# Token rows gathered to partitions 0 to 31 and 64 to 95 with a 128-entry index column, in a mixture-of-experts kernel

## The chip, the cores and the metric

The kernel runs on one core of a Trainium2 chip. Engines are named as in the profile: PE is TensorE's matmul, PEld its weight load, DVE is VectorE, ACT ScalarE, POOL GpSimd, SP SyncE. Sixteen DMA engines move data for the core. The metric is the device time of one execution in microseconds (us), as the median over several runs.

## The reference

Two transformer blocks over 512 tokens of width 1024, in float32. The first has sparse and differential attention and an MLP. The second has windowed attention, an mLSTM branch and, at its end, a mixture of 32 experts. Only this last part is touched:

```python
# each token picks one group of 8 experts and its 2 best experts in it
order = jnp.argsort(expert_ids)              # 1024 assignments, sorted by expert
...
xs = xt[row_tok].reshape(nblk, MOE_BLOCK, D) # rows of the normed input h
def expert_block(args):
    xb, e = args
    return (jax.nn.silu(xb @ w_gate[e]) * (xb @ w_up[e])) @ w_down[e]
...
y = jnp.zeros((T, D)).at[row_tok].add(ys * row_w[:, None])
```

Each expert has 6.3 MB of weights: `gate` and `up` (1024 x 512 each) and `down` (512 x 1024).

## The kernel before

The first 1,220 us, about, hold everything ahead of the experts. The router then sorts the 1024 assignments into blocks of 64 places (`BLK`), one block per expert and a second one for up to four experts: 36 blocks (`STATIC`), worked through in the order of the list `ORDER`. A block is seldom full. Its tokens stand on consecutive places, whose start turns by 5 places from block to block (`TURN`).

**Tables.** `place_choice` (DVE) builds one-hot matrices, `place_hot` (place of each assignment in its block) and `tok_weight` (block, with the token's number minus 1024, and its weight). `all_slots` (PE, line 1629) multiplies them and gets, for each of the 64 places and each block, the token number and the gate weight in PSUM. `all_rows` (DVE, lines 2968, 2914 and 2915) copies the weights to `slot_weight` and makes `row_ids`: the token number, or for an empty place a number beyond the last token.

**Gather.** For each block from the third on, POOL copies one column of `row_ids` to `idcol` (line 929) and issues an indirect DMA (line 921), which fetches one row of 4 KB from `h_scratch` in HBM for each index into `xs[0:64, s]` (the tile is `stage`; s is 0 or 1 in turn). An index out of bounds fetches nothing. The gather of block n+5 is issued when PE has turned the rows of block n+3, and the first three ahead of the loop. The first two blocks are made by matmuls, without a gather.

**Blocks.** For block n PE computes gate and up (line 1641: `xsT` with 1024 x 512 weights, the two products in the two halves of PE's columns), turns the gathered rows of block n+1 (line 1635, `turn_tokens`, partitions 0 to 95 of `xs` into 96 columns of PSUM, of which DVE's `turned_tokens` takes columns 0 to 63), computes down for block n-1 (line 1658), and turns the hidden rows (line 1649). DVE line 2982 makes the hidden rows. ACT lines 2121 and 2123 write the result rows to `ys` (the tile is `smb`).

**Scatter.** `add_rows` (POOL, line 943) adds the 64 rows of `ys` to the output in HBM with an accumulating indirect DMA. One is issued per block, each after the one before has landed. For the last block, `spread` issues another gather ahead of the last scatter, for a loop over overflow blocks, which does not run with these inputs.

**Weights.** SP streams the experts' weights through eleven places of 2 MB in the order of `LOADS`, each as soon as PE has used up the piece that lay there. All go through one queue, q1 in the profile. POOL's indirect DMAs go through q0.

Of the kernel before, what the change touches and what calls it, by code (L numbers as in the profile page):

```python
# [23 lines left out]
I32 = mybir.dt.int32  # L24
ALU = mybir.AluOpType
# [3 lines left out]
P = 128  # L29
D = 1024  # L30
SEQ = 512
NT = SEQ // P
# [15 lines left out]
BLK = 64  # L48
# [8 lines left out]
STATIC = NE + DOUBLES  # L57
BLOCKS = STATIC + MAXJOBS + 2
# [51 lines left out]
def build(nc, io, out):  # L110
    ctx = ExitStack()
    with ctx:
        def sb(name, shape, dt=F32):
            return ctx.enter_context(nc.sbuf_tensor(name, shape, dt))
# [5 lines left out]
        ps = ctx.enter_context(nc.psum_tensor("ps", [P, 8, 512], F32))  # L120
# [30 lines left out]
        small = sb("small", [P, 640])  # L151
        cur = [0]
# [14 lines left out]
        row_gain = col(KT)  # L167
# [122 lines left out]
        wpos = sb("wpos", [P, 2, NT])  # L290
        tokid = sb("tokid", [P, 2, NT])
        iot = sb("iot", [P, 2 * BLK + 1])
        idcol = sb("idcol", [BLK, 4], I32)
        tables = fmask[0:1, 0:MAXJOBS + NE].bitcast(I32)
        jobs, placed = tables[:, 0:MAXJOBS], tables[:, MAXJOBS:]
        njobs = sb("njobs", [1, 1], I32)
# [29 lines left out]
        place_hot = gb[:, 0:2 * NT * BLK].rearrange("p (n r) -> p n r", n=2 * NT)  # L326
        tok_weight = flat_s[:, 0:4 * NT * BLOCKS].rearrange("p (n b) -> p n b", n=2 * NT)
# [3 lines left out]
        xs = stage  # L331
        ys = flat_s[0:64, :].rearrange("p (s d) -> p s d", s=2)
        xsT = [v.rearrange("p (k t) -> p k t", k=KT) for v in (gb[:, 512:1024], cmask[:, :])]
        hidT = ptb[:, 1, 0:256].rearrange("p (k t) -> p k t", k=4)
        slot_weight = ptb[64:128, 1, 256:256 + BLOCKS]
        sgate, hid = flat_s[64:128, 1024:1536], flat_s[64:128, 1536:2048]

        row_ids = small[0:BLK, cur[0]:cur[0] + BLOCKS].bitcast(I32)
        id_work = small[0:BLK, cur[0] + BLOCKS:cur[0] + 2 * BLOCKS]
        assert cur[0] + 2 * BLOCKS <= 640  # L340

        h_dram = nc.dram_tensor("h_scratch", (SEQ, D), F32, kind="Internal").ap()
# [82 lines left out]
        idT_done, ids_ready, job_ready = sem("idT_done"), sem("ids_ready"), sem("job_ready")  # L425
# [6 lines left out]
        idcol_ready = sem("idcol_ready")  # L432
# [33 lines left out]
        b = C_P2  # L466
# [340 lines left out]
        def _(pool):  # L807
# [110 lines left out]

            def gather_tokens(s):
                pool.sem_inc(fetches, 1)  # L920
                pool.indirect_dma_start(out=xs[0:BLK, s, :], out_offset=None, in_=h_dram,
                                        in_offset=bass.IndirectOffsetOnAxis(ap=idcol[:, s:s + 1], axis=0),
                                        bounds_check=SEQ - 1, oob_is_err=False).then_inc(gather[s], 16)

            nth = [0]

            def index_column(col_, b):
                nth[0] += 1
                pool.tensor_copy(idcol[:, col_:col_ + 1], row_ids[:, b:b + 1]).then_inc(idcol_ready, 1)
                pool.wait_ge(idcol_ready, nth[0])  # L930

            def block_at(n):
                return ORDER[n][1] if n < STATIC else n

            def fetch(n, s, turned):
                if turned > 0:
                    pool.wait_ge(ex["xt"], turned)
                index_column(s, block_at(n))
                gather_tokens(s)

            def add_rows(s):
                pool.sem_inc(fetches, 1)
                pool.indirect_dma_start(out=out[0], out_offset=bass.IndirectOffsetOnAxis(ap=idcol[:, 2 + s:3 + s], axis=0),
                                        in_=ys[0:BLK, s, :], in_offset=None, bounds_check=SEQ - 1, oob_is_err=False,
                                        compute_op=ALU.add).then_inc(rows_out, 16)

            def spread(n):
                last = n == STATIC - 1
                if last:
                    pool.wait_ge(rows_out, 16 * (n - 1))  # L950
                    index_column(2 + n % 2, block_at(n))
                    fetch(STATIC + 1, 0, STATIC - 1)
                    pool.wait_ge(last_rows, 1)
                pool.wait_ge(ex["ys"], n + 1)
                if not last:
                    index_column(2 + n % 2, block_at(n))
                if n:
                    pool.wait_ge(rows_out, 16 * n)
                add_rows(n % 2)

            for n in range(2, 5):
                fetch(n, n % 2, n - 3)
            pool.wait_ge(out_store, 16 * NT)
            for n in range(STATIC):
                spread(n)
                if n + 5 <= STATIC:
                    fetch(n + 5, (n + 5) % 2, n + 2)
            base = nth[0]
            pool.wait_ge(job_ready, 1)
            n = pool.value_load(njobs[0:1, 0:1], min_val=0, max_val=MAXJOBS)  # L970
            with pool.If(n > 0):
                with pool.Fori(0, n) as j:
                    pool.wait_ge(ex["xt"], j + STATIC)
                    pool.tensor_copy(idcol[:, 0:1], row_ids[:, bass.ds(j + (STATIC + 2), 1)]).then_inc(idcol_ready, 1)
                    pool.wait_ge(idcol_ready, j * 2 + (base + 1))
                    gather_tokens(0)
                    pool.wait_ge(ex["ys"], j + (STATIC + 1))
                    pool.tensor_copy(idcol[:, 2:3], row_ids[:, bass.ds(j + STATIC, 1)]).then_inc(idcol_ready, 1)
                    pool.wait_ge(idcol_ready, j * 2 + (base + 2))
                    pool.wait_ge(rows_out, j * 16 + 16 * STATIC)  # L980
                    add_rows(0)
# [3 lines left out]
        def _(pe):  # L985
# [80 lines left out]
            for g in range(BESIDE1):  # L1066
                if G1[g][0] != "wi":
                    dense1(g, (0, 1))
                else:
                    group(bank1(g), wi_done, 1)  # L1070
                    pe.wait_ge(swap_done, 5)
                    for i in range(NT):
                        ins = pe.transpose(ps[:, bank1(g), 8 * i:8 * i + 8], wi_rows[:, i * P:(i + 1) * P],
                                           ident[64:72, 64:72])
# [77 lines left out]
            for a in range(N_STEPS + 3):  # L1152
# [8 lines left out]
                if piece(a):  # L1161
                    g, part = piece(a)
# [346 lines left out]
            for half in range(2):  # L1509
# [5 lines left out]
                for j in range(4):  # L1515
                    for br_ in range(2):
                        bank = (2 * bo + br_) % 4
                        group(bank, u_done, bo + 1)
                        for k in range(4):
                            ins = pe.matmul(ps[:, bank, :],  # L1520
                                            ring[c % 2][:, br_ * 2048 + k * 512 + j * P:br_ * 2048 + k * 512 + (j + 1) * P],
                                            yT[:, 4 + k, :] if br_ else oT[:, k, :], start=(k == 0), stop=(k == 3))
# [82 lines left out]
            for k in range(KT):  # L1605
                for i in range(NT):
                    ins = pe.matmul(ps[:, k // 4, (k % 4) * P:(k % 4 + 1) * P], x[:, i, k * P:(k + 1) * P],
                                    first_hot[:, 2 * i:2 * i + 2, :], start=(i == 0), stop=(i == NT - 1))
# [4 lines left out]
            for i in range(NT):  # L1613
                ins = pe.matmul(ps[:, 3, 0:3], first_hot[:, 2 * i:2 * i + 2, :].rearrange("p e r -> p (e r)"), r_first_w[:, i, :],
                                start=(i == 0), stop=(i == NT - 1))
# [9 lines left out]
            def all_slots():  # L1625
                for c in range(2):
                    pe.wait_ge(slots_ready, c + 1)
                    for n in range(NT * c, NT * (c + 1)):
                        ins = pe.matmul(ps[0:BLK, 7, 0:2 * BLOCKS], place_hot[:, n, :], tok_weight[:, n, :],
                                        start=(n == 0), stop=(n == 2 * NT - 1))  # L1630
                ins.then_inc(idT_done, 1)

            def turn_tokens(s):
# [43 lines left out]
            for n, (q, _) in enumerate(ORDER):  # L1677
                s = n % 2
# [28 lines left out]
            n = pe.value_load(njobs[0:1, 0:1], min_val=0, max_val=MAXJOBS)  # L1707
# [436 lines left out]
        def _(dve):  # L2144
            steps = [0]

            def then(ins):

                steps[0] += 1
                ins.then_inc(dv, 1)  # L2150
                dve.wait_ge(dv, steps[0])

            def bc(col_, n):

                return col_.unsqueeze(len(col_.shape)).broadcast_to(list(col_.shape) + [n])
# [682 lines left out]
            root(3)  # L2838
            dve.wait_ge(root_ready, NT)

            dve.memset(r_two[:, 0:FIXED], 0.0)
            dve.tensor_copy(r_near[:, 0:FIXED], iot[:, 0:FIXED])
            dve.tensor_scalar(block_start, iot[:, 0:BLOCKS], float(BLK), None, ALU.mult)
# [66 lines left out]
                                         ps[:, half, :].rearrange("p (k t) -> p k t", k=4)[:, :, 0:BLK],  # L2910
                                         bc(gcol[:, 6, 4 * half:4 * half + 4], BLK), ALU.mult)

            def token_ids(dst, src, work_):
                then(dve.tensor_scalar(work_, src, float(-SEQ), float(-SEQ), ALU.is_ge, ALU.mult))
                return dve.scalar_tensor_tensor(out=dst, in0=src, scalar=float(2 * SEQ), in1=work_, op0=ALU.add, op1=ALU.add)

            cnt = ps[:, 7, 0:NE]
            then(dve.tensor_tensor(more, bc(cnt, NBLK - 1), block_start[:, 1:NBLK].unsqueeze(1).broadcast_to([P, NE, NBLK - 1]),
                                   ALU.is_gt))
# [45 lines left out]
            dve.sem_inc(job_ready, 1)  # L2965
            def all_rows():
                dve.wait_ge(idT_done, 2)
                dve.tensor_copy(slot_weight, ps[0:BLK, 7, BLOCKS:2 * BLOCKS])
                token_ids(row_ids, ps[0:BLK, 7, 0:BLOCKS], id_work).then_inc(ids_ready, 1)

            def turned_tokens(s, n):
                dve.wait_ge(ex["xt"], n)
                for half in range(2):
                    ins = dve.tensor_tensor(xsT[s][:, 4 * half:4 * half + 4, :],
                                            ps[:, half, 0:4 * 96].rearrange("p (k t) -> p k t", k=4)[:, :, 0:BLK],
                                            bc(row_gain[:, 4 * half:4 * half + 4], BLK), ALU.mult)
                ins.then_inc(ex["xT"], 1)

            def hidden(e, weight):
# [81 lines left out]
```

## Time and profile before

| | |
|---|---|
| median of 3 runs | 1709.47 us (1708.0 to 1710.34) |
| span of the profiled execution | 1706.2 us |
| own time of that execution | not on the page; the median is 3.3 us above the span |
| PE busy | 1639.4 us (96%) |
| DVE, ACT, POOL busy | 736.9, 388.6, 189.6 us |
| q1 (weights) | 287.40 MB, 43.9% of 16 engines' span |
| q0 (POOL's DMAs) | 12.90 MB, 3.7% |

The span runs from the first to the last instruction of the profiled execution. A queue's share is the time that its packets took, over 16 DMA engines and the stretch that is looked at. It is a mean over stages: in the last 450 us the DMA engines are far busier than over the whole span.

### The profile page before, as it was taken

The page shows a single profiled execution, that of the slowest core. Times are in us where ns is not written, and L with a number is a line of the kernel's source. Part 1 is how long each engine was busy: PE and PEld are TensorE (multiplying, and loading weights), DVE is VectorE, ACT ScalarE, POOL GpSimd, SP SyncE. Part 2 cuts the span into 40 slices and gives each one's busy share as a digit, 9 for nine tenths or more (in the row PEclk, how much of TensorE's full clock was granted, in tenths as well). Part 3 has the DMA queues.
Part 4 walks back from the last instruction along what each step waited for, and adds up shares of the span by engine and source line. Part 5 has one row for each costly group of instructions (what it writes and reads, how often), then busy time and mean ns, then how long its engine had stood idle before and what let it go on. Part 6 is the DMA issues. An engine that isn't in the chain of part 4 may idle for free.

```text
span 1706.2 us, 18047 instructions
## 1 busy us (share of the span) xinstructions
PE 1639.4 (96%) x6990; PEld 951.3 (56%) x6990; DVE 736.9 (43%) x1520; ACT 388.6 (23%) x823; POOL 189.6 (11%) x206
## 2 busy tenths in 40 slices
PE   7999999999999999999999999999999998988986
PEld 4444454578888888865444778645533333333332
DVE  3386886465444544452775355243422121111111
ACT  4443754410000000032454233102211111110110
POOL 1000000000000000010000414132022222111211
PEclk9999999999999999999999999999999999999998
DMA  5531114030222122222111113647899999999996
GB/s 186 126 72 49 50 50 148 1 111 1 99 99 88 61 99 99 99 63 99 50 50 50 50 50 99 201 148 281 315 384 395 401 402 403 395 396 412 395 404 239
DMA packets 72257, 303.61 MB, mean 178 GB/s; under 512 B 10669, under 2 KB 11826, under 8 KB 59756
## 3 DMA queue, kind: packets, MB, share of 16 engines
q1 hardware_dynamic: 63856, 287.40, 43.9%
q0 software_dynamic: 7568, 12.90, 3.7%
q10 hardware_dynamic: 748, 2.15, 0.3%
q8 instruction: 56, 0.92, 0.2%
q14 instruction: 29, 0.24, 0.0%
HBM read 297.56 MB, written 15.73 MB: 184 GB/s over the span
## 4 chain that ended last, share of the span: by engine, by line
PE 87%; DMA 9%; DVE 2%; issue 1%; another core or an unknown queue 0%; ACT 0%; POOL 0%; POOLq 0%; SPq 0%; DVEq 0%; ACTq 0%
PE ps L1193 11%; PE ps L1237 11%; PE ps L1641 11%; PE ps L1061 9%; DMA W<-in_w_expert_up 8%; PE ps L1334 7%; PE ps L1658 6%; PE ps L1481 5%; PE ps L1097 3%; PE ps L1057 3%; PE ps L1520 3%; PE ps L1546 3%; PE ps L1345 2%; PE ps L1116 1%; PE ps L1635 1%; PE ps L1013 1%
## 5 line engine op out<-in xcount | busy, mean ns | idle before, releaser
L2982 DVE SCALAR_TENSOR_TENSOR smb<-smb,ptb,ps 64x512 f32<-64x512 f32 x34 | 38.3, 1126 | 291.6 <-ACT smb L2115 291.6
L1641 PE MATMUL ps<-W,gb 128*64 128x512 f32 x480 | 140.3, 645 | 15.9 <-DMA W<-in_w_expert_up 15.9
L1061 PE MATMUL ps<-W 128*128 128x512 f32 (+1 forms) x336 | 149.3, 596 | 1.4 <-DVE W L2172 1.4
L1641 PE MATMUL ps<-W,cmask 128*64 128x512 f32 x480 | 129.3, 599 | 6.1 <-DMA W<-in_w_expert_up 3.1
L1334 PE MATMUL ps<-W 128*128 128x512 f32 x272 | 124.0, 606 | 1.9 <-DVE yT L2630 1.9
L1193 PE MATMUL ps<-yT,W 128*128 128x256 f32 x512 | 113.0, 379 | 0.0
L1658 PE MATMUL ps<-W,ptb 128*64 128x512 f32 x464 | 107.7, 606 | 1.4 <-DVE ptb L2988 1.4
L1237 PE MATMUL ps<-W,mix 128*128 128x256 f32 x496 | 108.5, 379 | 0.0
L1193 PEld LDWEIGHTS ps<-yT,W 128*128 128x128 f32 x512 | 97.3, 190 | 13.2
L1061 PEld LDWEIGHTS ps<-W 128*128 128x128 f32 (+1 forms) x336 | 61.2, 188 | 74.9 <-issue 72.9
L1237 PEld LDWEIGHTS ps<-W,mix 128*128 128x128 f32 x496 | 94.2, 190 | 12.8
L1237 PE MATMUL ps<-W 128*128 128x256 f32 x400 | 88.0, 379 | 0.0
L1334 PEld LDWEIGHTS ps<-W 128*128 128x128 f32 x272 | 50.6, 192 | 66.4 <-issue 63.5
L1641 PEld LDWEIGHTS ps<-W,gb 128*64 128x64 f32 x480 | 43.0, 148 | 78.8 <-issue 78.2
L1868 ACT ACTIVATE smb<-ps 128x512 f32<-128x512 f32 x10 | 6.0, 596 | 349.8 <-PE ps L1237 185.3
L1193 PE MATMUL ps<-W 128*128 128x256 f32 x384 | 85.5, 379 | 0.0
L1237 PEld LDWEIGHTS ps<-W 128*128 128x128 f32 x400 | 76.0, 190 | 10.3
L2115 ACT ACTIVATE smb<-ps 64x512 f32<-64x512 f32 x34 | 20.1, 590 | 261.9 <-PE ps L1641 261.9
L1641 PEld LDWEIGHTS ps<-W,cmask 128*64 128x64 f32 x480 | 42.7, 137 | 65.0 <-issue 64.3
L1193 PEld LDWEIGHTS ps<-W 128*128 128x128 f32 x384 | 72.8, 190 | 9.8
L1658 PEld LDWEIGHTS ps<-W,ptb 128*64 128x64 f32 x464 | 31.3, 138 | 55.5 <-issue 50.8
L1794 ACT ACTIVATE yT<-ps 32x512 f32<-32x512 f32 x82 | 48.3, 589 | 44.2 <-PE ps L1061 43.4
(476 smaller groups left out, 2426.3 us busy)
## 6 DMA issues: line engine op xcount, KB each, us to landing
W<-in_w_expert_up SPq DMA_DIRECT2D x27, 2048.0 KB, 40.7
W<-in_w_expert_gate SPq DMA_DIRECT2D x24, 2048.0 KB, 37.6
W<-in_w_expert_down SPq DMA_DIRECT2D x24, 2048.0 KB, 44.4
W<-in_w_in SPq DMA_DIRECT2D x16, 2048.0 KB, 7.7
W<-in_w_up SPq DMA_DIRECT2D x8, 2048.0 KB, 8.2
W<-in_w_down SPq DMA_DIRECT2D x8, 2048.0 KB, 7.9
W<-in_w_out SPq DMA_DIRECT2D x4, 2048.0 KB, 7.9
yT<-in_w_expert_down SPq DMA_DIRECT2D x4, 2048.0 KB, 39.8
```

Source lines behind the costliest of these rows:

```text
L1057: ins = pe.matmul(ps[:, bank, :], hT[:, k, j * P:(j + 1) * P], wv[:, k, :], start=(k == 0), stop=(k == KT - 1))
L1061: ins = pe.matmul(ps[0:n, bank, :], wv[:, k, j * P:j * P + n], hT[:, k, :], start=(k == 0), stop=(k == KT - 1))
L1097: ins = pe.matmul(ps[:, bank, :], lhs[:, k, i * P:(i + 1) * P], ring_view(c, KT, 512)[:, k, :], start=(k == 0), stop=(k == 7))
L1193: ins = pe.matmul(ps[:, bank, 256 * j:256 * j + 256], lhs[:, k, j * P:(j + 1) * P], rhs[:, k, :], start=(j == 0 and k == 0), stop=(j == 1 ...
L1237: ins = pe.matmul(ps[:, bank, 256 * t:256 * t + 256], lhs[:, k, t * P:(t + 1) * P], rhs[:, k, :], start=(q == 0 and t == 0 and k == 0), st ...
L1334: ins = pe.matmul(ps[:, bank, :], wv[:, k, j * P:(j + 1) * P], hT[:, k, :], start=(k == 0), stop=(k == KT - 1))
L1481: ins = pe.matmul(ps[:, bank, 256 * j:256 * j + 256], lhs[:, k, j * P:(j + 1) * P], rhs[:, k, :], start=(j == 0 and k == 0), stop=(j == 1 ...
L1520: ins = pe.matmul(ps[:, bank, :], ring[c % 2][:, br_ * 2048 + k * 512 + j * P:br_ * 2048 + k * 512 + (j + 1) * P], yT[:, 4 + k, :] if br_ ...
L1546: ins = pe.matmul(ps[:, bank, :], lhs[:, k, t * P:(t + 1) * P], rhs[:, k, :], start=(k == 0), stop=(k == 3))
L1641: ins = pe.matmul(ps[64 * part:64 * part + 64, 2, :], xsT[s][:, k, :], w[part][:, k, :], start=(k == 0), stop=(k == KT - 1))
L1658: ins = pe.matmul(ps[64 * half:64 * half + 64, 4, :], hidT[:, k, :], w[:, k, half * 512:(half + 1) * 512], start=(k == 0), stop=(k == 3))
L1794: ins = act.activation(yT[32 * r:32 * r + 32, 4 + swaps % 2, :], ps[32 * (r ^ 1):32 * (r ^ 1) + 32, bank, :], ACT.Copy)
```

## The change

The gathers write 128 partitions' worth of entries instead of 64. Places 0 to 31 of a block go to partitions 0 to 31, places 32 to 63 to partitions 64 to 95. The entries for partitions 32 to 63 and 96 to 127 hold an index out of bounds, so nothing is fetched for them. For this `all_slots` computes the two halves of the places into two groups of PSUM partitions, `all_rows` works on the two groups apart (`gather_ids`, filled with 1024 beforehand) and copies them together for the scatter (`row_ids`) and the weights. DVE takes columns 0 to 31 and 64 to 95 of the turned rows. The scatter is as before, from 64 partitions.

```diff
@@ tiles @@
-        idcol = sb("idcol", [BLK, 4], I32)
+        idcol = sb("idcol", [P, 4], I32)
...
-        row_ids = small[0:BLK, cur[0]:cur[0] + BLOCKS].bitcast(I32)
-        id_work = small[0:BLK, cur[0] + BLOCKS:cur[0] + 2 * BLOCKS]
+        gather_ids = small[:, cur[0]:cur[0] + BLOCKS].bitcast(I32)
+        id_work = small[:, cur[0] + BLOCKS:cur[0] + 2 * BLOCKS]
+        row_ids = small[0:BLK, cur[0] + BLOCKS:cur[0] + 2 * BLOCKS].bitcast(I32)
@@ POOL @@
-                pool.indirect_dma_start(out=xs[0:BLK, s, :], out_offset=None, in_=h_dram,
+                pool.indirect_dma_start(out=xs[:, s, :], out_offset=None, in_=h_dram,
                                         in_offset=bass.IndirectOffsetOnAxis(ap=idcol[:, s:s + 1], axis=0),
                                         bounds_check=SEQ - 1, oob_is_err=False).then_inc(gather[s], 16)
...
-            def index_column(col_, b):
+            def token_column(s, b):
                 nth[0] += 1
-                pool.tensor_copy(idcol[:, col_:col_ + 1], row_ids[:, b:b + 1]).then_inc(idcol_ready, 1)
+                pool.tensor_copy(idcol[:, s:s + 1], gather_ids[:, b:b + 1]).then_inc(idcol_ready, 1)
+                pool.wait_ge(idcol_ready, nth[0])
+
+            def row_column(s, b):
+                nth[0] += 1
+                pool.tensor_copy(idcol[0:BLK, 2 + s:3 + s], row_ids[:, b:b + 1]).then_inc(idcol_ready, 1)
                 pool.wait_ge(idcol_ready, nth[0])
...
             pool.wait_ge(out_store, 16 * NT)
+            pool.wait_ge(ids_ready, 2)
             for n in range(STATIC):
                 spread(n)
@@ PE @@
                     for n in range(NT * c, NT * (c + 1)):
-                        ins = pe.matmul(ps[0:BLK, 7, 0:2 * BLOCKS], place_hot[:, n, :], tok_weight[:, n, :],
-                                        start=(n == 0), stop=(n == 2 * NT - 1))
+                        for part in range(2):
+                            ins = pe.matmul(ps[64 * part:64 * part + 32, 7, 0:2 * BLOCKS], place_hot[:, n, 32 * part:32 * part + 32],
+                                            tok_weight[:, n, :], start=(n == 0), stop=(n == 2 * NT - 1))
@@ DVE @@
+            dve.tensor_scalar(gather_ids, iot[:, 0:BLOCKS], 0.0, float(2 * SEQ), ALU.mult, ALU.add)
...
             def all_rows():
                 dve.wait_ge(idT_done, 2)
-                dve.tensor_copy(slot_weight, ps[0:BLK, 7, BLOCKS:2 * BLOCKS])
-                token_ids(row_ids, ps[0:BLK, 7, 0:BLOCKS], id_work).then_inc(ids_ready, 1)
+                quarters = (slice(0, 32), slice(64, 96))
+                for at in quarters:
+                    ins = dve.tensor_scalar(id_work[at], ps[at, 7, 0:BLOCKS], float(-SEQ), float(-SEQ), ALU.is_ge, ALU.mult)
+                then(ins)
+                for at in quarters:
+                    ins = dve.scalar_tensor_tensor(out=gather_ids[at], in0=ps[at, 7, 0:BLOCKS], scalar=float(2 * SEQ), in1=id_work[at],
+                                                   op0=ALU.add, op1=ALU.add)
+                ins.then_inc(ids_ready, 1)
+                dve.wait_ge(ids_ready, 1)
+                for part, at in enumerate(quarters):
+                    dve.tensor_copy(slot_weight[32 * part:32 * part + 32], ps[at, 7, BLOCKS:2 * BLOCKS])
+                    ins = dve.tensor_copy(row_ids[32 * part:32 * part + 32], gather_ids[at])
+                ins.then_inc(ids_ready, 1)
...
                 for half in range(2):
-                    ins = dve.tensor_tensor(xsT[s][:, 4 * half:4 * half + 4, :],
-                                            ps[:, half, 0:4 * 96].rearrange("p (k t) -> p k t", k=4)[:, :, 0:BLK],
-                                            bc(row_gain[:, 4 * half:4 * half + 4], BLK), ALU.mult)
+                    ins = dve.tensor_tensor(xsT[s][:, 4 * half:4 * half + 4, :].rearrange("p k (q t) -> p k q t", q=2),
+                                            ps[:, half, 0:4 * 96].rearrange("p (k q t) -> p k q t", k=4, q=3)[:, :, 0:3:2, :],
+                                            bc(bc(row_gain[:, 4 * half:4 * half + 4], 2), 32), ALU.mult)
```

On POOL, behind the last of the router's helper sums and up to the second scatter, the kernel before has these instructions (line, operation, destination and sources, shape):

```order
L929 COPY idcol<-small 64x1
L921 DMA stage<-h_scratch,idcol 64x1024
L929 COPY idcol<-small 64x1
L921 DMA stage<-h_scratch,idcol 64x1024
L929 COPY idcol<-small 64x1
L921 DMA stage<-h_scratch,idcol 64x1024
L929 COPY idcol<-small 64x1
L943 DMA out_x<-smb,idcol 512x1024
```

In the changed kernel they are:

```order
L930 COPY idcol<-small 128x1
L922 DMA stage<-h_scratch,idcol 128x1024
L930 COPY idcol<-small 128x1
L922 DMA stage<-h_scratch,idcol 128x1024
L930 COPY idcol<-small 128x1
L922 DMA stage<-h_scratch,idcol 128x1024
L935 COPY idcol<-small 64x1
L949 DMA out_x<-smb,idcol 512x1024
```

The order is the same, and the gathers and their index columns have 128 entries. The same pattern goes on through the loop.

On DVE, behind the second `place_choice` and ahead of the second block's hidden rows, there are in the kernel before (`ptb` holds `slot_weight`, `small` the ids):

```order
L2997 TENSOR_TENSOR gb<-ptb,iot 128x256
L2968 COPY ptb<-ps 64x54
L2914 TENSOR_SCALAR small<-ps 64x54
L2915 SCALAR_TENSOR_TENSOR small<-ps,small 64x54
L2982 SCALAR_TENSOR_TENSOR smb<-smb,small,ps 64x128x4
```

and in the changed kernel:

```order
L3013 TENSOR_TENSOR gb<-ptb,iot 128x256
L2975 TENSOR_SCALAR small<-ps 32x54 x2
L2978 SCALAR_TENSOR_TENSOR small<-ps,small 32x54 x2
L2983 COPY ptb<-ps 32x54
L2984 COPY small<-small 32x54
L2983 COPY ptb<-ps 32x54
L2984 COPY small<-small 32x54
L2998 SCALAR_TENSOR_TENSOR smb<-smb,small,ps 64x128x4
```

Three operations become eight. The ids now come ahead of the weights' copies.

On PE, between the first block's down and the second block's gate and up, the kernel before has

```order
L1658 MATMUL ps<-W,ptb 64x512 x8
L1629 MATMUL ps<-smb,gb 64x108 x8
L1641 MATMUL ps<-W,cmask 64x512 x16
```

and the changed kernel

```order
L1666 MATMUL ps<-W,ptb 64x512 x8
L1637 MATMUL ps<-smb,gb 32x108 x16
L1649 MATMUL ps<-W,cmask 64x512 x16
```

`all_slots` has twice as many matmuls of half the width, at the same place.

## Rows read from the trace of the kernel before

**Rows 1.** Page: its first line.

```profile
span 1706.2 us, 18047 instructions
```

**Rows 2.** Stretch 1500 to 1550: length, busy engines, clock, DMA share, GB/s.

```profile
1500.00:1550.00 50.00, 40.29 (x200) 15.76 (x196) 7.74 (x15) 6.52 (x11) 9.92 (x15) 0.97 1.02 406
```

**Rows 3.** PE's waits from 1238 us on: total us, times, longest.

```profile
PE ps L1641 <- DMA W<-in_w_expert_up: 27.8, 11, 5.0
```

**Rows 4.** Chain that ended last, near the end: start, us, what.

```profile
1660.50 4.88 another core or an unknown queue
1665.51 9.21 PE ps L1641 x32
1679.66 7.02 PE ps L1641 x32
```

**Rows 5.** DMA queues from 1248 to 1672: packets, MB, share of 16 engines.

```profile
q1 hardware_dynamic: 11245, 161.84, 93.5%
q0 software_dynamic: 5155, 7.32, 7.3%
```

**Rows 6.** DMA queues from 1442 to 1447.

```profile
q1 hardware_dynamic: 147, 2.15, 100.3%
q0 software_dynamic: 10, 0.00, 0.1%
```

**Rows 7.** DMA queues from 1177 to 1183.

```profile
q1 hardware_dynamic: 178, 2.55, 100.0%
```

**Rows 8.** POOL from 1345 to 1352: start, us, what.

```profile
1345.37 0.99 POOL L921 DMA_INDIRECT stage<-h_scratch,idcol  x1 [0.86 <-POOL idcol L929]
1350.32 1.45 POOL L943 DMA_INDIRECT out_x<-smb,idcol  x1 [0.92 <-POOL idcol L929]
```

**Rows 9.** DMA queues from 1349 to 1354.

```profile
q1 hardware_dynamic: 94, 1.39, 83.9%
q0 software_dynamic: 74, 0.26, 15.9%
```

**Rows 10.** DMA queues from 1355 to 1359.

```profile
q1 hardware_dynamic: 99, 1.43, 84.2%
q0 software_dynamic: 79, 0.15, 19.6%
```

**Rows 11.** DMA queues from 358 to 361, POOL loading `gb`.

```profile
q1 hardware_dynamic: 499, 1.00, 87.0%
q0 software_dynamic: 50, 0.20, 18.5%
```

**Rows 12.** DMA queues from 1168 to 1173.

```profile
q1 hardware_dynamic: 991, 2.00, 104.9%
```

**Rows 13.** The same chain, two earlier pieces.

```profile
1190.69 1.02 PE ps L1575 x15
1227.92 1.38 PE ps L1629 x15
```

**Rows 14.** A stretch with DMA engines idle; SP's next issue.

```profile
1236.00:1237.00 1.00, 1.00 (x10) 0.70 (x8) 0.00 (x0) 0.68 (x1) 0.00 (x0) 1.00 0.00 0
1236.45 0.34 SPq L777 DMA_DIRECT2D W<-in_w_expert_gate  x1
```

**Rows 15.** Gathers into `stage`, 1225 to 1262: us from issue to landing.

```profile
DMA to landing us min/median/max: 3.0/8.7/9.7
```

**Rows 16.** Timeline: first gather's issue on POOL, its reader on PEld.

```profile
1231.31 1.06 POOL L921 DMA_INDIRECT stage<-h_scratch,idcol  x1 [0.96 <-POOL idcol L929]
1236.19 0.70 PEld L1635 LDWEIGHTS ps<-ident,stage 96*128 96x128 f32 x8 [0.81 <-DMA stage<-h_scratch,idcol]
```

**Rows 17.** Timeline from 1696 us: ACT and POOL.

```profile
1696.23 0.59 ACT L2121 ACTIVATE smb<-ps 64x512 f32<-64x512 f32 x1 [3.85 <-PE ps L1658]
1696.28 1.01 POOL L921 DMA_INDIRECT stage<-h_scratch,idcol  x1 [0.90 <-POOL idcol L929]
1698.05 1.42 POOL L943 DMA_INDIRECT out_x<-smb,idcol  x1 [0.76 <-issue]
```

More of the change, by code:

```diff
@@ L937, in fetch @@
                     pool.wait_ge(ex["xt"], turned)
-                index_column(s, block_at(n))
+                token_column(s, block_at(n))
                 gather_tokens(s)
@@ L942, in add_rows @@
                 pool.sem_inc(fetches, 1)
-                pool.indirect_dma_start(out=out[0], out_offset=bass.IndirectOffsetOnAxis(ap=idcol[:, 2 + s:3 + s], axis=0),
+                pool.indirect_dma_start(out=out[0], out_offset=bass.IndirectOffsetOnAxis(ap=idcol[0:BLK, 2 + s:3 + s], axis=0),
                                         in_=ys[0:BLK, s, :], in_offset=None, bounds_check=SEQ - 1, oob_is_err=False,
@@ L950, in spread @@
                     pool.wait_ge(rows_out, 16 * (n - 1))
-                    index_column(2 + n % 2, block_at(n))
+                    row_column(n % 2, block_at(n))
                     fetch(STATIC + 1, 0, STATIC - 1)
@@ L955, in spread @@
                 if not last:
-                    index_column(2 + n % 2, block_at(n))
+                    row_column(n % 2, block_at(n))
                 if n:
@@ L973, in _ @@
                     pool.wait_ge(ex["xt"], j + STATIC)
-                    pool.tensor_copy(idcol[:, 0:1], row_ids[:, bass.ds(j + (STATIC + 2), 1)]).then_inc(idcol_ready, 1)
+                    pool.tensor_copy(idcol[:, 0:1], gather_ids[:, bass.ds(j + (STATIC + 2), 1)]).then_inc(idcol_ready, 1)
                     pool.wait_ge(idcol_ready, j * 2 + (base + 1))
@@ L977, in _ @@
                     pool.wait_ge(ex["ys"], j + (STATIC + 1))
-                    pool.tensor_copy(idcol[:, 2:3], row_ids[:, bass.ds(j + STATIC, 1)]).then_inc(idcol_ready, 1)
+                    pool.tensor_copy(idcol[0:BLK, 2:3], row_ids[:, bass.ds(j + STATIC, 1)]).then_inc(idcol_ready, 1)
                     pool.wait_ge(idcol_ready, j * 2 + (base + 2))
@@ L2911, in first_rows @@
                                          bc(gcol[:, 6, 4 * half:4 * half + 4], BLK), ALU.mult)
-            def token_ids(dst, src, work_):
-                then(dve.tensor_scalar(work_, src, float(-SEQ), float(-SEQ), ALU.is_ge, ALU.mult))
-                return dve.scalar_tensor_tensor(out=dst, in0=src, scalar=float(2 * SEQ), in1=work_, op0=ALU.add, op1=ALU.add)
             cnt = ps[:, 7, 0:NE]
```

## The prediction

> **What bounds the kernel now.** First the stage in which the change acts. The experts run from about 1220 us to the end. Here the 16 DMA engines are never free: a stretch of it shows a DMA share of 1.01, while PE works 40 of 50 us [rows 2]. Then who waits: PE stands 27.8 us in 11 waits at line 1641 for `up` weights [rows 3], and the chain that ended last passes through such a wait of 4.88 us at 1660.50 [rows 4] and then holds nothing but the last two blocks, some 30 us of PE work, and their scatters. So the arrival of the last weights sets the end. A microsecond less of work per DMA engine before 1660 is a microsecond off the span, until PE's waits are used up.
>
> Next, what that work is. From 1248 to 1672 us q1, the weights, moved 161.84 MB at 93.5% [rows 5]. I turn such a row into engine time per MB: share x stretch x 16 engines / MB. The stage as a whole: 0.935 x 424 x 16 / 161.84 = 39.2 us. Where POOL moves no rows it is 1.003 x 5 x 16 / 2.15 = 37.3 [rows 6], and at another such place 37.6 [rows 7]. So 1.6 to 1.9 us per MB, 259 to 307 us of engine time, are lost to something. POOL's timeline shows candidates, a gather issued at 1345.37 and a scatter at 1350.32 [rows 8]. Their packets come some microseconds behind their issue. In the stretch of the gather q1 took 0.839 x 5 x 16 / 1.39 = 48.3 us per MB beside 0.26 MB of q0, which are 64 rows of 4 KB [rows 9]. In the stretch of the scatter it took 0.842 x 4 x 16 / 1.43 = 37.7 [rows 10], all but undisturbed. So a gather slows the weights beside it by almost 30%, and an accumulating scatter, which reads partitions 0 to 63 and writes HBM, does not. The disturbance belongs to writing rows into the partitions of `stage`. The one load of POOL that fills all 128 partitions beside q1 shows the other side: q1 took 0.870 x 3 x 16 / 1.00 = 41.8 us per MB beside it [rows 11] (packets of 2 KB there), and a stretch of the same packets with no q0 took 42.0 [rows 12]. With destinations spread over 128 partitions nothing is lost.
>
> The Trainium skill has a mechanism for this. SBUF — State Buffer, "Door 1: The DMA port swizzle", says that partitions 0 to 63 lie behind 8 of 16 ports and 64 to 127 behind the other 8, with p and p+32 behind the same one. DMA: Bandwidth & Descriptors, "The descriptor swizzle", says that in a transfer to 128 partitions each DMA engine writes the port that is its own, four partitions and the four 32 above them. By these two, 64 rows on partitions 0 to 63 crowd 16 engines onto 8 ports, and 128 entries with rows in 0 to 31 and 64 to 95 give every engine four rows, all behind its own port. No row of this trace names an engine or a port; the rates above agree with it.
>
> **The change part by part.**
>
> 1. *Weights beside gathers.* From below: the gather's stretch lost (48.3 - 37.4) x 1.39 = 15.1 us for 64 rows [rows 9], 0.24 us a row. The scatters and gathers of the stage moved 7.32 MB, 1,787 rows [rows 5], half of them gathered: 890 x 0.24 = 210 us, or 13.1 per engine. From above: the whole excess, 259 to 307, less what scatters take ((37.7 - 37.4) x 1.43 x 36 = 15), is 244 to 292, or 15 to 18. I take 15.5, the lower edge of the second way: it misses no gather, and the first rests on one sample. If the disturbance stays, this is 0.
>
> 2. *The rows themselves.* A gathered row took 0.159 x 80 / 64 = 0.20 us [rows 9], one of the undisturbed load 0.185 x 48 / 50 = 0.18 [rows 11]. Between 0 and 0.04 less for 890 rows gives 0 to 2.2 per engine. I take 1.5.
>
> 3. *More packets.* Each gather gets 64 more entries, all out of range. Today's out-of-range entries and semaphores are the small packets of q0: 10 took 0.001 x 80 = 0.08 us [rows 6], 8 to 10 ns each. 64 x 34 gathers x 10 ns / 16 = 1.4 us more. From below it is nothing, if such an entry leaves no packet; the other bound is double.
>
> 4. *PE's `all_slots`.* 8 matmuls of 64 columns of weights become 16 of 32. The old ones took 1.38 us for 15 records [rows 13], 92 ns each. If a half costs as much as a whole, that is 1.5 us more; if the two halves overlap entirely, nothing. The nearest row is the router's pair of products, which also alternate between two column groups: 1.02 us for 15, 68 ns each at 128 moving columns [rows 13]. 32 x 62 ns = 2.0 against 16 x 92 = 1.5: 0.5 more. It counts in full, though the stage is DMA's: the DMA engines stand empty at 1236, and SP issues the next piece at 1236.45 [rows 14], when PE has finished block 1's gate and up products, which come behind `all_slots`. From there on pieces pile up: a block's three pieces of 2.1 MB take 3 x 2.1 x 39.2 / 16 = 15.4 us, more than PE needs for its block (7.02 us for gate and up [rows 4], and less than that for the rest).
>
> 5. *DVE.* Three small operations of `all_rows` become eight, the first gather's indices ready after four of them. DVE then has nothing to do until block 1's products are done, at about 1236 [rows 16], so it costs the engine nothing. What is behind it is POOL's first gather, issued at 1231.31 [rows 16] and landed 3.0 us later, the shortest such time [rows 15], at 1234.3. Its reader came to it at 1235.4 and started at 1236.19 [rows 16], so the margin is 1.1 to 1.9 us. A delay of some 0.2 here and a longer issue (below, 0 to 1.0) fit into it. Beyond it each us would delay PE. I take 0. The 128-row fill of `gather_ids` lies among DVE's router work behind nobody, well under 1 us, 0. The new pattern of `turned_tokens` writes as many elements as before and lies beside PE's `down` products: 0.
>
> 6. *POOL.* A gather's issue takes 0.99 us with 64 entries [rows 8]; with 128 it lies between that and double. In the loop nothing feels it: gathers land 8.7 to 9.7 us after issue [rows 15] and are read two blocks, over 14 us of products [rows 4], after their buffer was free. At the end it is bare. The last gather, which fetches no valid row, stands ahead of the last scatter: it runs from 1696.28 for 1.01 us, the scatter follows at 1698.05, and the last rows were ready at 1696.82 [rows 17]. So whatever the issue gains in length comes on top of the end, 0 to 1.0. I take 0.5.
>
> 7. *Uneven load.* A block's tokens lie on consecutive slots. [...] Between 0 and 2; I take 0.5.
>
> The sum: -15.5 - 1.5 + 1.4 + 0.5 + 0.5 + 0.5 = -14.1 us. The profiled execution spans 1706.2 [rows 1] and the median is 1709.5, so 3.3 lie outside the span in either kernel. 1692.1 of span, **1695.4 us**. PE's 27.8 us of waits leave room for it. One bonus is in the range only: the 32 products after the last wait took 9.21 us where the same group without a wait ahead takes 7.02 [rows 4], so a shorter wait may give back up to 2.2.
>
> **The rivals.**
>
> *The disturbance is not where the rows land (1712).* Gathers also read `h_scratch` in HBM, a narrow region. If its reading slows the weights, moving the destination changes nothing and only the costs stay: 1.4 + 0.5 + 0.5 = +2.4. Against it: the accumulating scatter reads rows of HBM too, as many bytes, and takes 0.196 x 64 / 37 = 0.34 us a row [rows 10] while q1 hardly slows. The skill's DMA: Bandwidth & Descriptors, "Where 436 GB/s comes from", would speak for it with its rule that a load from HBM is bound by HBM at about 358 GB/s per core; the trace does not agree, q1 alone moves 2.15 MB in 5 us, 430 GB/s [rows 6]. Chance 0.10.
>
> *Half of it (1703).* The gather moves entries to engines otherwise than the plain load does, so that only some rows meet a free path, or the DMA engines run dry at places where PE has not freed a buffer. Half of terms 1 and 2, 8.5, less 2.9, is -5.6. Chance 0.13.
>
> *Slower (1723).* The place is how 128 entries are dealt to 16 DMA engines. If by eights in order, the used partitions 0 to 31 and 64 to 95 belong to eight engines: 890 rows x 0.20 = 178 us on 8 engines is 22.2 each in place of 11.1, on the engines that then deliver last, and the disturbance stays. +11.1 + 2.4 = +13.5. It decides against the kernel as soon as the used engines are fewer than about 13. For it speaks that no gather of 128 entries is in the trace; against it the undisturbed 128-partition load of POOL [rows 11]. Chance 0.09.
>
> **How the numbers follow.** The forecast (11 to 19 us gained) has 0.65, more than that 0.03, the half 0.13. The bounds of terms 1 to 7 give the likeliest case a range of 1689 to 1701. With the half the range is 1687 to 1707. What a measurement of this kernel can tell from no change is about 0.2%, 3.4 us: faster 0.81, same 0.10 (the first rival), slower 0.09.
>
> **What would show it.** Right: in a gather's stretch q1 stays at 37 to 38 us per MB, the stage's mean falls from 39.2 to under 38.2, and PE's waits for `up` fall to half. q0 holds 64 more packets per gather. `all_slots` shows 32 records in about 2 us, gathers issue in 1.0 to 2.0 us. Wrong: q1 still at 45 or more beside a gather, or gathers that last longer than today's 5 us.

## The result

The changed kernel takes **1690.58 us** (median of 4 runs, 1688.85 to 1694.38) beside 1709.47 us before (median of 4 runs, 1708.0 to 1710.34). The ratio is 0.9888 with a 95% interval of 0.9874 to 0.9901, so it is faster by 17 to 22 us. The profiled execution took 1690.63 us, with a span of 1688.7.

The page's first line:

```profile
span 1688.7 us, 18085 instructions
```

The weights' queue over the experts' stage, the answer to [rows 5]; the span is 17.5 us shorter now, so the stretch ends earlier, at 1650:

```profile
q1 hardware_dynamic: 11057, 160.26, 93.6%
```

By the prediction's own reckoning this is 0.936 x 402 x 16 / 160.26 = 37.6 us of engine time per MB of weights, where it was 39.2. It is the figure of the places without gathers, 37.3 to 37.6 [rows 6, 7]: the disturbance is gone, not halved. The stretch of the same gather of 64 rows, now 1348 to 1352, the answer to [rows 9]:

```profile
q1 hardware_dynamic: 103, 1.43, 83.3%
q0 software_dynamic: 75, 0.26, 16.1%
```

0.833 x 4 x 16 / 1.43 = 37.3 us per MB beside the 0.26 MB of rows, where it was 48.3. The rows took 0.161 x 64 / 64 = 0.16 us each, where it was 0.20.

PE's waits from 1238 us on, the answer to [rows 3] (line 1649 is the former 1641, line 1666 the former 1658):

```profile
PE ps L1649 <- DMA W<-in_w_expert_up: 17.8, 7, 4.3
PE ps L1666 <- DMA W<-in_w_expert_down: 1.2, 1, 1.2
```

17.8 us of these waits for `up` are left of 27.8, more than the half that the prediction named as a sign of being right. Most of the rest of the gain shows in the products: PE's busy time fell from 1639.4 to 1631.9 us, because products that come behind a wait are longer (9.21 us in place of 7.02 for 32 of them, [rows 4]) and there are fewer such waits. The one wait for `down` is the last block's. The chain that ended last, which before held nothing but PE's work and the scatters from 1665.38 on, now passes through the very last piece of weights (start, length, what):

```profile
1626.52 43.13 DMA W<-in_w_expert_down
```

It lands at 1669.65, 19 us before the end. The DMA engines' share is as it was, 1.02 (length, busy engines, clock, DMA share, GB/s of a stretch), the answer to [rows 2]:

```profile
1500.00:1550.00 50.00, 44.72 (x221) 17.36 (x219) 8.80 (x15) 5.90 (x10) 9.93 (x15) 0.97 1.02 417
```

The stage is still bound by its weights; the DMA engines only move 417 GB/s in place of 406.

The side costs. The chain that ended last at `all_slots` and at the first gather; POOL's issue of a gather in the loop; the reader of the first gather on PEld (idle time before it in brackets); the last gather and scatter (answers to [rows 13], [rows 8], [rows 16] and [rows 17]):

```profile
1226.70 1.63 PE ps L1637 x32
1230.45 6.25 DMA stage<-h_scratch,idcol
```

```profile
1344.72 1.04 POOL L922 DMA_INDIRECT stage<-h_scratch,idcol  x1 [0.86 <-POOL idcol L930]
1236.75 0.69 PEld L1643 LDWEIGHTS ps<-ident,stage 96*128 96x128 f32 x8 [2.31 <-DMA stage<-h_scratch,idcol]
1678.63 1.05 POOL L922 DMA_INDIRECT stage<-h_scratch,idcol  x1 [0.90 <-POOL idcol L930]
1680.51 1.45 POOL L949 DMA_INDIRECT out_x<-smb,idcol  x1 [0.83 <-issue]
```

`all_slots` takes 1.63 us for 32 records where 15 took 1.38. A gather's issue takes 1.04 us with 128 entries where it took 0.99 with 64. PEld stood idle 2.31 us ahead of the first gather's rows where it had stood 0.81. The chain shows why: from the start of its issue to its landing this gather took 6.25 us, so it landed at 1236.70, just ahead of its reader. In the kernel before, the answer for this gather alone (issued at 1231.31, [rows 16]) is:

```profile
DMA to landing us min/median/max: 4.6/4.6/4.6
```

At the end the scatter follows the gather's issue by 1.88 us, where it was 1.77.

**A measure for the experiments.** Ahead of the experts the code is the same in all kernels, but its length in the profiled executions is not. The first of PE's 18 products that stand between the router's logits and its ranks (line 1594 before) starts here before, and in the changed kernel here (the chain that ended last):

```profile
1193.86 7.80 PE ps L1594 x18
```

```profile
1192.94 7.80 PE ps L1601 x18
```

I call what is left of the span from there the experts' part: 1706.2 - 1193.9 = 512.3 us before and 1688.7 - 1192.9 = 495.8 in the changed kernel, 16.5 less. Of the 17.5 us between the spans about 1 therefore lies where nothing was changed.

### The profile page after: what moved, and what is told of

Its sections match the earlier page's. It is cut to its first block, busy times and chain, and to the rows that moved or that the text cites. A ratio compares the mean times of both kernels' runs of the same rounds, so it can differ in the third digit from the quotient of the medians.

```text
span 1688.7 us, 18085 instructions
## 1 busy us (share of the span) xinstructions
PE 1631.9 (97%) x7006; PEld 947.6 (56%) x7006; DVE 737.7 (44%) x1526; ACT 387.8 (23%) x823; POOL 192.7 (11%) x206
## 3 DMA queue, kind: packets, MB, share of 16 engines
q0 software_dynamic: 9872, 12.91, 3.7%
## 4 chain that ended last, share of the span: by engine, by line
PE 85%; DMA 11%; DVE 2%; issue 1%; ACT 0%; POOL 0%; SPq 0%; POOLq 0%; DVEq 0%; ACTq 0%
PE ps L1200 11%; PE ps L1244 11%; PE ps L1649 9%; PE ps L1068 9%; DMA W<-in_w_expert_up 8%; PE ps L1341 7%; PE ps L1488 6%; PE ps L1666 5%; PE ps L1104 3%; PE ps L1064 3%; PE ps L1527 3%; PE ps L1553 3%; DMA W<-in_w_expert_down 3%; PE ps L1352 2%; PE ps L1123 1%; PE ps L1020 1%
## 5 line engine op out<-in xcount | busy, mean ns | idle before, releaser
L1649 PE MATMUL ps<-W,gb 128*64 128x512 f32 x480 | 132.7, 611 | 6.3 <-DMA W<-in_w_expert_up 6.3
```

The costliest lines, as they stand in the source:

```text
L1649: ins = pe.matmul(ps[64 * part:64 * part + 64, 2, :], xsT[s][:, k, :], w[part][:, k, :], start=(k == 0), stop=(k == KT - 1))
```

## The experiments

Three theories stood against each other. No view of the profile names a DMA engine or an SBUF port, so what follows tells them apart by rates and times. **Own port**: a gathered row disturbs the weights when the DMA engine that writes it writes behind an SBUF port that another engine's weights use, and a gather of 128 entries is dealt so that each engine stays behind its own. **Spread**: it only matters whether the rows fall on 8 ports or on 16. **HBM**: it is the reading of the rows that disturbs. The first turns on which engine writes a row, the second on where the rows lie.

**128 entries, rows on partitions 0 to 63.** The kernel before with this:

```diff
-                pool.indirect_dma_start(out=xs[0:BLK, s, :], ...
+                pool.indirect_dma_start(out=xs[:, s, :], ...
+            # idcol has 128 rows; the ids of partitions 64 to 127 are filled with 1024
```

> The kernel before with one thing taken from the change: the gathers have 128 entries, but the rows stay on partitions 0 to 63, and the entries for 64 to 127 are out of range. Own-port theory (a row disturbs the weights when a DMA engine writes it behind a port that is another engine's, and 128 entries are dealt so that each engine writes behind its own): q1 beside a gather stays at 37 to 39 us of engine time per MB, but all rows fall to 8 of 16 engines, 890 rows x 0.16 = 142 us, 17.8 each in place of 8.9, so 1695 to 1701 us. Spread theory (what counts is whether the rows fall on 8 or on 16 ports): disturbed as before, q1 at about 48 beside a gather, 1709 to 1713 us. HBM theory (the reading of the rows disturbs): the same 1709 to 1713, and it can then not explain the changed kernel.

Measured: 1700.43 us, ratio 0.9941 (0.9924 to 0.9957). The weights' queue from 1250 to 1650:

```profile
q1 hardware_dynamic: 11039, 159.36, 93.4%
```

0.934 x 400 x 16 / 159.36 = 37.5 us per MB: nothing is disturbed, though every row lands where it landed before and was read where it was read before. So neither the place of the rows nor their reading is the cause, and spread and HBM fall. The time shows the other half of the theory. The experts' part is 1698.6 - 1194.4 = 504.2 us, 8.4 above the changed kernel's. By the theory all rows fall to half the engines, which costs 890 x 0.16 / 16 = 8.9 more on these. The end of the stage shows that half. From 1665 to 1675, with no row under way:

```profile
q1 hardware_dynamic: 220, 2.07, 48.7%
```

For 10 us just half of the 16 engines' time is taken by weights, as it is when half of the engines still have pieces left and the other half have none. In the changed kernel q1's share falls from 99.5% (1660 to 1665) through 60.6% to 12.4% (1670 to 1675), without such a plateau.

**The changed kernel's places, dealt by two gathers of 32 entries.**

```diff
-                pool.indirect_dma_start(out=xs[:, s, :], ... ap=idcol[:, s:s + 1] ...
+                for at, ids in ((slice(0, 32), idcol), (slice(64, 96), high_col)):
+                    pool.indirect_dma_start(out=xs[at, s, :], ... ap=ids[0:32, s:s + 1] ...
+            # high_col holds the indices of places 32 to 63 on partitions 0 to 31
```

> The changed kernel with each gather of 128 entries cut into two gathers of 32 entries, one to partitions 0 to 31 and one to 64 to 95. The rows land where they land in the changed kernel, but 32 entries are dealt otherwise to 16 engines, two each. Own-port theory: the weights are disturbed again, q1 at 45 or more per MB beside a gather, and the gain is lost: 1706 to 1713 us. Spread theory: the places are as in the changed kernel, q1 at 37 to 39, 1690 to 1694 us (1 us of it for one more issue on POOL ahead of the last scatter).

Measured: 1715.16 us, ratio 1.0031 (1.0020 to 1.0043). From 1250 to 1650, and beside 64 gathered rows, 1351 to 1356:

```profile
q1 hardware_dynamic: 10458, 152.31, 93.5%
```

```profile
q1 hardware_dynamic: 100, 1.41, 85.3%
q0 software_dynamic: 94, 0.26, 16.6%
```

The stage is at 0.935 x 6400 / 152.31 = 39.3 us per MB, the rows' stretch at 0.853 x 5 x 16 / 1.41 = 48.4. These are the figures of the kernel before, with the rows in the changed kernel's places. This is the second half of the proof against spread: with the same rows in the same places, what counts is how many entries a gather has. The time is 2 us above what I had allowed. Its experts' part is 518.1, 5.8 over the kernel before. 0.7 of it is one more issue of 0.93 us on POOL ahead of the last scatter (2.50 us from the last gather's first issue to the scatter's, in place of 1.77); the rest I did not follow.

**96 entries.**

```diff
-                pool.indirect_dma_start(out=xs[:, s, :], ... ap=idcol[:, s:s + 1] ...
+                pool.indirect_dma_start(out=xs[0:96, s, :], ... ap=idcol[0:96, s:s + 1] ...
```

> The changed kernel with gathers of 96 entries (partitions 0 to 95) in place of 128; the rows land on 0 to 31 and 64 to 95 as in the changed kernel. Own-port theory, if the entries are dealt by the port of their partition whatever their number: q1 undisturbed, 1690 us, less 0.6 for 32 fewer small packets a gather. Own-port theory, if 96 entries are dealt otherwise (six to an engine): engines write behind others' ports, q1 at 42 or more beside a gather, 1700 to 1712 us. I expect the second. A theory that needs only the places of the rows, which the run of two gathers of 32 entries has already spoken against, says 1690.

Measured: 1709.27 us, ratio 0.9998 (0.9989 to 1.0008). From 1250 to 1650:

```profile
q1 hardware_dynamic: 10513, 153.05, 93.4%
```

0.934 x 6400 / 153.05 = 39.1 us per MB, and the experts' part is 1710.1 - 1196.3 = 513.8. The whole gain hangs on the number of entries: the last 32, which fetch nothing, are what makes it.

**The rows 32 partitions higher**, on 32 to 63 and 96 to 127, in a gather of 128 entries (PE's table products and DVE's columns move with them):

```diff
-                quarters = (slice(0, 32), slice(64, 96))
+                quarters = (slice(32, 64), slice(96, 128))
...
-    pe.transpose(ps[:, k // 4, (k % 4) * 96:(k % 4 + 1) * 96], xs[0:96, s, k * P:(k + 1) * P], ident[0:96, 0:96])
+    pe.transpose(ps[:, k // 4, (k % 4) * P:(k % 4 + 1) * P], xs[:, s, k * P:(k + 1) * P], ident[:, :])
```

> The changed kernel with its rows 32 partitions higher: the 128-entry gathers fetch rows for partitions 32 to 63 and 96 to 127, the entries for 0 to 31 and 64 to 95 are out of range. PE turns 128 partitions in place of 96, which is 32 more columns in 8 products a block, hidden where PE waits for weights. Own-port theory in full (p and p + 32 lie behind the same port and fall to the same DMA engine): q1 undisturbed at 37.5 us per MB over the stage, 1690 to 1693 us. If only the first four entries of each engine were dealt by its own port, or if the twins lay behind other ports: disturbed, 39 us per MB or more, 1700 to 1711 us.

Measured: 1690.93 us, ratio 0.9898 (0.9878 to 0.9918), with the experts' part at 1688.5 - 1192.7 = 495.8 and q1 at 93.6% for 159.67 MB, 37.5 us per MB. It is the changed kernel in all these figures. The upper entries are as good as the lower, and the time shows no less even deal.

**No rows at all, before and after.** In both kernels each gather takes its indices from a block without tokens. So no row is fetched, and the experts from the third block on work on stale rows:

```diff
-                index_column(s, block_at(n))      # token_column in the changed kernel
+                index_column(s, BLOCKS - 1)
```

> The kernel before with all entries of its gathers out of range, so that no row is fetched and the experts from the third block on work on stale rows. It leaves out the rows' transfer and its disturbance alone. Own-port and spread theory: 8.9 us per engine for the rows themselves, 17.0 for the disturbance and 1.6 for the rows being slowed, 27.5 in all: 1682 us, if PE's waits of 31 us leave room. A theory in which the gain of the change came from elsewhere than the gathers would leave this at more than 1695.

> The changed kernel with all entries of its gathers out of range, so that no row is fetched and the experts from the third block on work on stale rows. All theories that put the disturbance on rows: the rows' own 8.9 us per engine go, so 1682 us. Beside the kernel before with the same cut it shows the fixed costs of the change alone: 1.2 us of small packets, 0.3 of the table products: 1 to 2 us above it. If the change had another gain than the undisturbed rows, it would stand below it.

Measured: 1679.84 us (1682 expected) for the kernel before without rows (ratio 0.9823, 0.9806 to 0.9839), and 1681.53 for the changed one without rows (0.9835, 0.9818 to 0.9851). From 1250 to 1650, before without rows and then changed without rows:

```profile
q1 hardware_dynamic: 11441, 163.06, 95.6%
q0 software_dynamic: 5121, 3.76, 5.3%
```

```profile
q1 hardware_dynamic: 11395, 162.70, 95.4%
q0 software_dynamic: 7173, 3.78, 5.6%
```

Both are at 37.5 us per MB, the figure that the changed kernel has with its rows. The experts' parts are 485.8 us in both. So rows cost 26.5 us in the kernel before (512.3 - 485.8) and 10.0 in the changed one (495.8 - 485.8). The page of the kernel before without rows also counts them:

```profile
q0 software_dynamic: 7568, 9.09, 3.1%
```

With rows q0 moved 12.90 MB, so 3.81 MB or 930 rows were gathered. Their own transfer is 930 x 0.161 / 16 = 9.4 us of the 10.0, which leaves about 0.6 for an uneven deal. The fixed costs of the change are 0 by the experts' parts and 1.7 by the medians, whose lowest and highest runs do not overlap (1679.40 to 1680.25, and 1681.36 to 1682.51). The packets of the out-of-range entries can be read from q0 above: 2,052 more of them took (0.056 - 0.053) x 400 = 1.2 us of each engine, to within 0.4 by the rounding of the shares.

**The first gather, cut in two.** The changed kernel with only its first gather in two parts of 32 entries, and the changed kernel again, unchanged:

```diff
+                if first:                      # the gather of the third block only
+                    for at, ids in ((slice(0, 32), idcol), (slice(64, 96), high_col)):
+                        pool.indirect_dma_start(out=xs[at, s, :], ... ap=ids[0:32, s:s + 1] ...
+                    return
```

> The changed kernel with its first gather alone cut into two of 32 entries; all others have 128. In the changed kernel PE stood 2.31 us ahead of the first gather's reader, where 0.81 is usual. If the nine packets per DMA engine (eight entries and a semaphore), each in turn with one of the weights, are what makes it late, three or four packets per part land sooner, PE's wait falls by about 1 us, and the time by up to 1 us beside the changed kernel: 1689.5 to 1690.5. If the lateness comes from the second issue on POOL or from DVE's added work, the wait stays or grows: 1691 to 1692.

> The changed kernel again, unchanged, as the measure for the run with a cut first gather on the same chip: 1689 to 1693 us by every theory, and 2.3 us ahead of the first gather's reader.

Measured: 1690.05 us (0.9888, 0.9871 to 0.9904) and 1691.23 us (0.9895, 0.9878 to 0.9911). The intervals do not part them. The readers of the first gather, in the cut one and in the repeated one (start, length, what, idle time before):

```profile
1235.93 0.70 PEld L1653 LDWEIGHTS ps<-ident,stage 96*128 96x128 f32 x8 [1.81 <-DMA stage<-h_scratch,high_col]
```

```profile
1238.06 0.69 PEld L1643 LDWEIGHTS ps<-ident,stage 96*128 96x128 f32 x8 [2.42 <-DMA stage<-h_scratch,idcol]
```

The wait shrank from 2.42 to 1.81 us, and the experts' parts are 1688.3 - 1192.7 = 495.6 and 1689.7 - 1194.2 = 495.5. The 0.6 us saved ahead of the first rows do not reach the end. A reason, argued: SP issued its next two pieces at 1235.19 and 1235.63, before that reader started, and from then on the DMA engines, not PE, set the pace.

## Why the prediction was right

The way, the size and the mechanism as far as the runs reach it were right: gathered rows slowed the weights beside them, and in a gather of 128 entries they no longer do. 18.9 us lie between the medians and 16.5 between the experts' parts, where 14.1 was forecast. The measured time lies inside the range and inside the forecast case of 11 to 19 us, though for the medians at its edge. Step by step:

1. *Weights beside gathers*, 15.5 forecast. Measured (39.2 - 37.5) x 162 / 16 = 17.2 of engine time. I had taken the lower edge of "all excess less the scatters'", 15 to 18; the middle would have met it.
2. *The rows themselves*, 1.5 forecast: (0.20 - 0.161) x 890 / 16 = 2.2. The rows gathered are 930, not 890, by the run without rows; the 890 left out those of the first gathers and took half of all rows for gathered.
3. *More packets*, 1.4: q0 has 2,304 packets more (9,872 in place of 7,568), which is 64 for each of 36 gathers. In the stretch of the runs without rows, which has 2,052 of them, they took 1.2 of engine time. All fixed costs together cost between 0 and 1.7 us.
4. *`all_slots`*, 0.5: 0.25. The halves overlap more than the 62 ns a record that the prediction took, which no row gives (its row has 68): it is 51.
5. *DVE and the first gather*, 0: the step failed in its reasoning, and that it did little harm is luck. The margin of 1.1 to 1.9 us came from a misread row: 3.0 us is the shortest of the landings in [rows 15], and it belongs to the second gather. The first landed 4.6 us after the start of its issue, at 1235.9, 0.3 before its reader started. In the changed kernel it took 6.3, 1.7 more, and PEld waited 1.5 longer. DVE's added operations are not the reason, for the issue starts 37.5 us after the start of the experts' part in both kernels. Nor is a longer issue (1.13 us in place of 1.06). Nor is the number of entries alone, for in the runs without rows the first gather landed after 4.2 us with 128 entries and after 5.1 with 64. With all rows on half the engines it took 7.0. That points to the most rows that one engine has to write, up to four now, in turn with packets of weights; this is argued and not shown. The cut first gather shows that 0.6 us of this wait cost nothing; for the rest it isn't shown.
6. *POOL's issue*, 0.5: 0.05 in the loop and 0.11 between the last gather and the last scatter. The pair of 32 entries took 0.95 and 0.90 us in the loop, so by far the most of it does not depend on the number of entries.
7. *Uneven load*, 0.5: about 0.6, what the runs without rows leave. How 64 entries were dealt to the engines no run shows, so the 0.5 rested on no row.

The runs without rows give a second sum, in time in place of engine time. All that hangs on rows (steps 1, 2 and 7) was to give -16.5, and gave 10.0 - 26.5 = -16.5. The fixed costs (steps 3, 4 and 6) were to be 2.4 and were 0. By this sum the 2.4 us that the experts' part was missed by are the costs. By engine time (steps 1 and 2) the gains were 2.4 larger than forecast. The two do not agree to better than some 2 us: by engine time the rows of the kernel before would cost 17.2 + 930 x 0.20 / 16 = 28.8, and 26.5 was measured. The 512.3 of the kernel before is from one execution; the changed kernel's 495.8 came again within 0.3 in three other runs.

The medians were missed by 4.8, 2.4 more. About 1 of it lies in the unchanged code ahead, whose length varies by over 4 us among the profiled executions (1192.6 to 1197.0). The other 1.4 is a step of the prediction: it put 3.3 us outside the span in either kernel, and in the changed one it is 1690.58 - 1688.7 = 1.9. In the executions on record that have both, time and span lie 1.8 to 1.9 apart; so the profiled one of the kernel before, at a span of 1706.2, was faster than the median.

Of the rivals, HBM was at odds with the accumulating scatter from the start, and the run with 128 entries on partitions 0 to 63 ended it. The slower one asked how 128 entries are dealt. The answer is not by eights in order: then the changed kernel's rows would be on 8 engines and would cost it what the rows on 0 to 63 cost. Entries 0 to 63 all fall to one half of the engines, as the 8.4 us and the 48.7% at the end of that run show, and those of 0 to 31 and 64 to 95 do not. The Trainium skill's rule for plain transfers to 128 partitions (DMA: Bandwidth & Descriptors, "The descriptor swizzle": engines 0 to 7 serve partitions 0 to 63, each with four and the four 32 above) says the same. For an indirect gather of 128 entries both this run and the one with the rows 32 higher agree with it.

What is shown is this: rows from gathers of 128 entries disturb nothing in three placements, rows from gathers of 32, 64 and 96 do, and neither the place of the rows, nor their reading, nor the out-of-range entries by themselves matter. That the reason is an engine writing behind another's port is not shown. A disturbance by any other trait of gathers of fewer than 128 entries would fit these runs as well. A gather of 128 entries dealt to the wrong engines would tell the two apart, and there was none.

## What to carry to other kernels

Read a queue's share together with its MB, as engine time per MB, beside and away from another queue's transfers. It shows a disturbance that the DMA share of 1.02 hides, and what it is worth. When indirect gathers run beside a saturated stream of 128-partition loads, give them 128 entries too, with the real rows on 0 to 31 and 64 to 95, so that both halves of the engines share the rows. Other small DMAs were not tried. Entries out of range are cheap in comparison: here 64 of them per gather came with 16.5 us of gain, and all fixed costs together were at most 1.7. Before a margin is taken from a minimum over several transfers, look up the one transfer that it is about. Half of the recipe is not enough: 128 entries with rows on 0 to 63 brought half the gain, and 96 entries nothing.

## What was not expected of the hardware

- A gather of 96 entries with the same rows in the same partitions as one of 128 disturbs the weights almost as much as one of 64 (39.1 us per MB against 37.5, and 39.2 before).
- 128 entries with rows on partitions 0 to 63 disturb nothing (37.5 us per MB) but cost 8.4 us, and q1 ends with 10 us at 48.7% of the engines.
- In the loop POOL's issue of an indirect gather takes 0.90 to 0.95 us with 32 entries, 0.99 with 64 and 1.04 with 128.
- The first gather landed 6.3 us after the start of its issue with 128 entries, where with 64 it had been 4.6, though the issue itself was only 0.07 longer. Without rows 128 entries landed after 4.2.
